# Two fused transformer blocks on one core: partial sums of squares on VectorE, a shorter final norm with stores in pieces, and the last layer's value tiles inside its scan

## The reference, cut to what matters

```python
# block 1, per layer i
mix = jnp.concatenate([conv_out, attn_out], axis=-1) @ w_out[i] + b_out[i]
h = layer_norm(DEEPNORM_ALPHA * h + mix, ln1_g[i], ln1_b[i])       # the norm "ln1_0", "ln1_1"
...
# block 2, per layer: x is the stream, ctx the context, 256 tokens each
xn = rmsnorm(x, norm_g) * (1 + scale_x) + shift_x                  # "rms0", "rms1"
cn = rmsnorm(ctx, norm_g) * (1 + scale_c) + shift_c
aq, ak, av, az, mq, mk, mv, mo, mz, mi, mf = project(xn, w_in)
caq, cak, cav, caz, cmq, cmk, cmv, cmo, cmz, cmi, cmf = project(cn, w_in)
att_x = window_ctx_attention(q, k, v, kc, vc, sink) * jax.nn.silu(az)
h_ctx, ctx_state = mlstm_bidir(cq, ck, cmv, cmi + b_i, cmf + b_f, mlstm_init_state(B))
h_lat, _ = mlstm_bidir(xq, xk, mv, mi + b_i, mf + b_f, ctx_state)
m_x = mlstm_post(h_lat, mo, mz, head_g)
x = x + gate_x * (jnp.concatenate([att_x, m_x], axis=-1) @ w_out)
...
return rmsnorm(x, final_g)                                         # "final"
```

## Time and profile before

| | |
|---|---|
| median of 3 runs | 2153.48 us (2153.09 to 2160.43) |
| the profiled execution's own time | 2151.44 us |
| its span in the trace | 2149.7 us |
| PE matmul busy | 2048.8 us, 95% |
| DVE, ACT busy | 777.3 us (36%), 406.5 us (19%) |
| mean DMA rate | 236 GB/s |
| last layer of block 2 in the trace | from about 1872 us to the end |

### The profile page before, as it was taken

How to read it: one execution, slowest core, us unless ns; L and a number is a source line. 1 busy time by engine, 2 the same in 40 slices (tenths; PEclk the granted TensorE clock), 3 DMA queues, 4 the chain that set the end, 5 groups by cost and what they waited for, 6 DMA issues and landing times.

```text
span 2149.7 us, 36889 instructions
## 1 busy us (share of the span) xinstructions
PE 2048.8 (95%) x15906; PEld 1484.5 (69%) x15906; DVE 777.3 (36%) x1764; ACT 406.5 (19%) x964; POOL 5.8 (0%) x12
## 2 busy tenths in 40 slices
PE   8999999999999999999999999998999898999877
PEld 6879999886776666666666656666645666576776
DVE  6737555595321111111011110113156355335354
ACT  1233110104210111000100000002143423123322
POOL 0000000000000000000000000000000000000000
PEclk9999999999999999999999999999999999999998
DMA  9483444545089999999999999993211111232100
GB/s 314 178 272 136 157 171 183 188 165 196 7 346 393 420 419 417 420 421 420 418 418 420 420 420 420 415 420 165 98 40 59 40 40 40 78 118 74 60 25 20
DMA packets 71940, 506.75 MB, mean 236 GB/s; under 512 B 7776, under 2 KB 9824, under 8 KB 11232
## 3 DMA queue, kind: packets, MB, share of 16 engines
q1 hardware_dynamic: 70624, 500.15, 58.2%
q0 software_dynamic: 1152, 4.19, 0.8%
HBM read 503.27 MB, written 1.05 MB: 235 GB/s over the span
## 4 chain that ended last, share of the span: by engine, by line
PE 89%; DMA 4%; DVE 4%; ACT 2%; issue 1%; DVEq 0%; SPq 0%; ACTq 0%
PE ps L450 87%; DMA work<-weights 2%; DMA ring<-weights 2%; PE ps L1161 1%; PE ps L724 1%; DVE work L2605 1%; ACT work L1771 0%; DMA xc<-x_t 0%; DVE work L2566 0%; PE ps L600 0%; DVE work L2672 0%; DVE work L2562 0%; DVE work L1955 0%; PE ps L1262 0%; DVE work L2563 0%
## 5 line engine op out<-in xcount | busy, mean ns | idle before, releaser
L450 PE MATMUL ps<-work 128*32 128x256 f32 (+8 forms) x5608 | 589.2, 383 | 30.9 <-DVE work L2605 11.3
L450 PE MATMUL ps<-work,ring 128*128 128x256 f32 (+2 forms) x2056 | 520.5, 408 | 6.1 <-DVE work L2672 5.0
L450 PEld LDWEIGHTS ps<-work 128*32 128x32 f32 (+3 forms) x5608 | 380.8, 138 | 196.8 <-issue 122.1
L450 PE MATMUL ps<-ring,work 128*32 128x256 f32 (+3 forms) x4824 | 470.4, 410 | 13.4 <-DMA work<-weights 4.0
L450 PEld LDWEIGHTS ps<-work,ring 128*128 128x128 f32 x2056 | 353.3, 192 | 142.6 <-issue 107.0
L450 PEld LDWEIGHTS ps<-ring,work 128*32 128x32 f32 (+1 forms) x4824 | 261.3, 120 | 148.2 <-issue 75.8
L450 PE MATMUL ps<-xc,ring 128*128 128x256 f32 (+1 forms) x1440 | 277.1, 352 | 5.6 <-DMA ring<-weights 4.0
L450 PEld LDWEIGHTS ps<-xc,ring 128*128 128x128 f32 x1440 | 241.7, 191 | 42.6 <-issue 7.5
L2218 DVE TENSOR_TENSOR work<-work,ps 128x256 f32<-128x256 f32 x42 | 17.7, 421 | 419.6 <-ACT work L1622 419.6
L450 PE MATMUL ps<-xc,work 128*128 128x256 f32 (+1 forms) x720 | 138.3, 350 | 0.0
L450 PEld LDWEIGHTS ps<-xc,work 128*128 128x128 f32 x720 | 120.8, 191 | 19.9 <-issue 3.8
(11 more groups left out here) (273 smaller groups left out, 1169.8 us busy)
## 6 DMA issues: line engine op xcount, KB each, us to landing
ring<-weights SPq DMA_DIRECT2D x317, 1024.0 KB, 12.2
work<-weights SPq DMA_DIRECT2D x154, 1024.0 KB, 16.2
work<-rel POOLq DMA_DIRECT2D x8, 512.0 KB, 9.3
con<-consts SPq DMA_DIRECT2D x1, 1368.0 KB, 21.2
xc<-x_t SPq DMA_DIRECT2D x1, 1024.0 KB, 7.7
xc<-ctx_t SPq DMA_DIRECT2D x1, 1024.0 KB, 25.2
out<-work SPq DMA_DIRECT2D x1, 1024.0 KB, 3.9
par<-params SPq DMA_DIRECT2D x1, 872.0 KB, 9.1
```

Source lines behind the costliest of these rows:

```text
L450: ins = eng.matmul(o, lhs, rhs, start=start, stop=stop, **kw)
```

## The change

Four edits.

1. **Norm ln1, both layers.** While DVE adds the residual (`block1_out`), it also adds up chunks 0 to 6 in `rstd1`, by six additions. PE's mean then takes 2 matmuls with ones, over that sum and over chunk 7, and not 8.
2. **Norms rms1 and final.** While DVE adds the output projection to x (`block2_out`), it also adds up the squares of chunks 0 to 6 in `rstd2`, by six additions, each placed ahead of the next chunk's addition. PE's sum of squares takes 2 matmuls and not 8.
3. **Final norm.** One operation for each chunk, (x * gain) * reciprocal, takes the place of a multiplication and a scaling: 8 operations and not 16. The store is 4 DMAs of 2 chunks (256 KB), each waiting only for its own chunks.
4. **The last layer's stream values.** In layer 1 the value tiles with t = 0, 1 (4 tiles, 8 pieces) leave the attention's filler and become the first filler of the scan. The attention deals 32 pieces and not 40; the scan 28 - 4 = 24 over its 24 steps, and not 16. The scan waits for the other four value tiles at its start, and for these at j = 2. The first `mz` tile of layer 1 uses bank 7.

```diff
+            def norm_mean_summed(l):
+                name = f"ln1_{l}"
+                o = fill(("mean", name), 0, (s["norm_centered"], before(name) + KC))
+                eng.wait_ge(s["res_summed"], (KC - 2) * (l + 1))
+                mm(o[:, 0:T], ones, rstd1, True, False)
+                eng.wait_ge(*source(name, KC - 1))
+                mm(o[:, 0:T], ones, res[:, KC - 1, :], False, True).then_inc(bank_full[0], 1)
+
+            def norm_var_summed(name, summed):
+                o = fill(("var", name), 1, (s["norm_std"], normk(name)))
+                eng.wait_ge(s["sq_summed"], summed)
+                mm(o[:, 0:T], ones, rstd2[:, 0:T], True, False)
+                eng.wait_ge(s["norm_squared"], before(name) + KC)
+                mm(o[:, 0:T], ones, squares(name, False)[:, KC - 1, 0:T], False, True).then_inc(bank_full[1], 1)
...
+        MV_FIRST = ([0, 1, 2, 3], [2, 3])
...
                 for u in range(2):
-                    w = next_unit()
-                    for t in range(4):
-                        o = fill(("mv", l, u, t), t % 2, (s["mv_copied"], 8 * l + 4 * u + t + 1))
+                    w = next_unit(beside=l == 1 and u == 1)
+                    if l:
+                        value_units.append(w)
+                    for k, t in enumerate(MV_FIRST[l]):
+                        o = fill(("mv", l, u, t), t % 2, (s["mv_copied"], 8 * l + len(MV_FIRST[l]) * u + k + 1))
                         yield from token_pieces(("mv", l, u, t), w, t, o, t % 2)
...
             def block2_third(l):
+                if l:
+                    for k in range(4):
+                        u, t = divmod(k, 2)
+                        b = 7 if k else 6
+                        o = fill(("mv", l, u, t), b, (s["mv_copied"], 8 * l + 4 + k + 1))
+                        yield from token_pieces(("mv", l, u, t), value_units[u], t, o, b)
...
-                    b = 7 if c else 6
+                    b = 7 if c or l else 6
...
-                rounds, total = att_rounds(l), 48 if l == 0 else 40
+                rounds, total = att_rounds(l), 48 if l == 0 else 32
...
-                total = (32 if l == 0 else 20) - SCAN_START[l]
+                total = (32 if l == 0 else 28) - SCAN_START[l]
...
-                eng.wait_ge(s["mv_copied"], 8 * (l + 1))
+                eng.wait_ge(s["mv_copied"], 8 * l + 2 * len(MV_FIRST[l]))
                 for j in range(4):
                     rows = has_rows(l, j, 0)
+                    if l and j == 2:
+                        eng.wait_ge(s["mv_copied"], 8 * (l + 1))
...
-            eng.wait_ge(s["norm_out"], outk("final"))
-            eng.dma_start(out, cen).then_inc(s["out_stored"], 16)
-            eng.wait_ge(s["out_stored"], 16)
+            for c in range(0, KC, 2):
+                eng.wait_ge(s["norm_out"], outk("final", c + 1))
+                eng.dma_start(out[:, c:c + 2, :], cen[:, c:c + 2, :]).then_inc(s["out_stored"], 16)
+            eng.wait_ge(s["out_stored"], 16 * KC // 2)
...
+            def final_norm():
+                eng.wait_ge(s["norm_std"], normk("final"))
+                link(eng.reciprocal(rstd2[:, 0:T], std2[:, 0:T]))
+                for c in range(KC):
+                    eng.scalar_tensor_tensor(out=cen[:, c, :], in0=xc[:, c, 0:T], scalar=par[:, PC("final_g", c)],
+                                             in1=rstd2[:, 0:T], op0=ALU.mult, op1=ALU.mult).then_inc(s["norm_out"], 1)
...
+                    if 1 <= c < KC - 1:
+                        eng.wait_ge(s["mix_added"], KC * l + c + 1)
+                        if c > 1:
+                            eng.wait_ge(s["res_summed"], (KC - 2) * l + c - 1)
+                        eng.tensor_tensor(rstd1, rstd1 if c > 1 else res[:, 0, :], res[:, c, :], ALU.add)\
+                            .then_inc(s["res_summed"], 1)
...
+            def sum_squares(l, c):
+                name = ("rms1", "final")[l]
+                had = (KC - 2) * l + c - 1
+                sq = squares(name, False)
+                eng.wait_ge(s["norm_squared"], before(name) + c + 1)
+                if c > 1:
+                    eng.wait_ge(s["sq_summed"], had)
+                eng.tensor_tensor(rstd2[:, 0:T], rstd2[:, 0:T] if c > 1 else sq[:, 0, 0:T], sq[:, c, 0:T], ALU.add)\
+                    .then_inc(s["sq_summed"], 1)
...
+                    if c >= 2:
+                        sum_squares(l, c - 1)
```

More of the change, by code:

```diff
@@ L305, in build @@
         names = """weights_used ones_loaded x_loaded params_loaded late_loaded rel_loaded rel_ready out_stored
-            norm_src norm_centered norm_squared norm_std norm_scaled norm_out norm_out_a coef_out
+            norm_src res_summed sq_summed norm_centered norm_squared norm_std norm_scaled norm_out norm_out_a coef_out
             cond_ready cond_row prep_done glu_gate glu_out qk_out v_out mod_out xo_half x_half conv_mixed
@@ L1116, in block2_second @@
                 for u in range(2):
-                    w = next_unit()
-                    for t in range(4):
-                        o = fill(("mv", l, u, t), t % 2, (s["mv_copied"], 8 * l + 4 * u + t + 1))
+                    w = next_unit(beside=l == 1 and u == 1)
[3 more added lines that the diff above has]
+                        o = fill(("mv", l, u, t), t % 2, (s["mv_copied"], 8 * l + len(MV_FIRST[l]) * u + k + 1))
                         yield from token_pieces(("mv", l, u, t), w, t, o, t % 2)
+            value_units = []
             def block2_third(l):
@@ L1380, in _ @@
                 block1_out(l)
-                norm(f"ln1_{l}", res, KC, T)
+                norm_mean_summed(l)
+                norm_var(f"ln1_{l}", KC, T, True)
                 if l == 0:
@@ L1394, in _ @@
                 if l:
-                    norm("rms1", xc, KC, T, centred=False)
+                    norm_var_summed("rms1", KC - 2)
                     context_var()
@@ L1402, in _ @@
                 block2_out(l, started)
-            norm("final", xc, KC, T, centred=False)
+            norm_var_summed("final", (KC - 2) * 2)
             assert unit_no[0] == UNITS, (unit_no[0], UNITS)
@@ L1727, in block2_second, with value_copy @@
                 for u in range(2):
-                    for t in range(4):
+                    for t in MV_FIRST[l]:
                         yield "mv", l, u, t
-                        o = tile(eng, "mv", l, u, t)
-                        eng.activation(mv[:, t, 2 * u:2 * u + 2, 0:M_DH],
-                                       o[:, 0:GW].rearrange("p (a b) -> p a b", b=M_DH), ACT.Copy)\
-                            .then_inc(s["mv_copied"], 1)
+                        value_copy(l, u, t)
+            def value_copy(l, u, t):
+                o = tile(eng, "mv", l, u, t)
+                eng.activation(mv[:, t, 2 * u:2 * u + 2, 0:M_DH], o[:, 0:GW].rearrange("p (a b) -> p a b", b=M_DH),
+                               ACT.Copy).then_inc(s["mv_copied"], 1)
             def block2_third(l):
@@ L1737, in block2_third @@
                 q_tiles = 4 if l == 0 else 2
+                if l:
+                    for u in range(2):
+                        for t in range(2):
+                            yield "mv", l, u, t
+                            value_copy(l, u, t)
                 for c in range(M_HEADS):
@@ L2799, in _ @@
                 block2_out(l)
-            norm("final", xc, KC, T,
-                 lambda c, a: eng.tensor_scalar(cen[:, c, :], cen[:, c, :], par[:, PC("final_g", c)], None, ALU.mult),
-                 centred=False, dst=cen)
+            final_norm()
 def weight_units(a):
```

## The result

| | before | after |
|---|---|---|
| median of the runs | 2161.10 us (16 runs, 2152.93 to 2176.41) | 2142.46 us (16 runs, 2131.82 to 2151.68) |
| the profiled execution and its span | 2151.44, 2149.7 us | 2139.72, 2137.7 us |

The ratio is 0.9913, with an interval of 0.9891 to 0.9935: faster by 0.9%, or 19 us. The time is 10 us over the one forecast and half a microsecond outside the range. Two things have to be kept apart: what the edits did, and how far the executions of one kernel lie apart. The executions of before cover 23 us, those of after 20 us. The gain itself, 18.6 us between the two medians with an interval of about 14 to 24, holds the 21.25 that was forecast.

The account below looks back on a forecast made before the run. The prediction took TensorE's work and waits as the bound. Norms and store 9.15 us, attention 12.1 and scan 0 sum to 21.25, so 2153.48 became 2132 us, range 2125 to 2142.

Parts of the forecast that it names:

- the base: Whole kernel: the median of before's runs, 2153.48 us, 2.0 above the profiled execution, from which the gain was subtracted.
- The sum: Whole kernel: norms and store 9.15 us, attention 12.1, scan 0, together 21.25 us saved.
- The additions on DVE: Norms: additions of about 0.41 us each hide beside PE's work; without that cover 0.41 at most would show.
- The end: Last square to the span's end: 14.1 us before, less 1.8, 1.6 and 1.0, gives 9.7 after.
- The store's term: Kernel's end: four stores for one save 1.0 us, between 0 and 1.9; by the Trainium skill 1.3.
- The attention: Layer 1 of block 2: eight pieces leave, waits grow 4.4 to 6.4 us, 99.8 becomes 87.7, 12.1 less.
- The scan: Last layer: exposed pieces cost 6.5 us, recovered clock returns 6.7; length stays 87.4 at granted clock 1.00.
- The price put on the filler's bank: Scan: exposed filler pieces wait for ACT's copy of shared bank 7, 0.65 us and 0.75 us.
- Rival 1: Scan: the low clock stays and 6.7 us of the gain is lost, 2139 us; chance 0.20.
- Rival 2: Scan grows by 12 us, eating the attention's gain; only 9.15 remains, 2144 us; chance 0.10.
- Rival 3: Experts: their weight stream ends when it did, losing ln1's 3.6 us, 2136 us; chance 0.10.
- Rival 4: Scan: new fillers keep TensorE at 1.2 GHz, making the kernel slower, 2172 us with half affected; chance 0.02.

Follow-up runs that it names:

- run 9: Kernel after plus one unread matmul in every second round of block 1's attention (12 in all): 2139.41 us median, 6 runs.
- run 11: Kernel before plus one unread matmul in every second round of block 1's attention (12 in all), sent again: 2161.55 us median, 12 runs.
- experiment 8: Kernel after with the result stored once as 1 MB instead of four 256 KB stores: 2149.65 us, one run; last square to end 10.67 us.
- Experiment 4: Kernel after with ACT copying the turned probabilities before a filler tile that ends with the round: 2122.87 us, ratio 0.9823 to before.
- run 6: Kernel before plus one unread matmul in every second round of block 1's attention (12 in all): 2160.32 us, ratio 0.9998.
- experiment 7: Kernel after with turned probabilities copied first, plus layer 1's scan filler tiles alternating between banks 6 and 7: 2125.33 us, ratio 0.9857 to before.
- run 1: Kernel before with only the fourth edit, the last layer's stream values computed in the scan: 2153.71 us, ratio 0.9936.
- run 10: Kernel after with turned probabilities copied first and 12 unread matmuls in block 1's attention: 2120.70 us, ratio 0.981 to before.
- experiment 12: Kernel after with turned probabilities copied first, no unread matmuls, sent again on another chip: 2134.66 us, ratio 0.9873 to before.
- run 5: Kernel before plus one unread matmul in every round of block 1's attention (22 in all): 2164.49 us, ratio 1.0015.

## Why the prediction was right and wrong

**The step that failed is the base.** "The median of the runs is 2.0 us above the profiled one, and I forecast 2153.48 - 21.25" takes three runs for the kernel's time, and allows "some 3 us between executions" in the range. Two of the three runs lay at the fast end: the 16 runs of before beside the result have a median of 2161.10, 7.6 us higher, and that is most of the 10.3 us by which the forecast missed; the other 2.6 lie in the gain, 18.6 for 21.25, and within its interval. The 85 runs of before in this study cover 2151.27 to 2177.97 with a median of 2162.4, and 20 of them are under 2156. From 2162.4 the same sum gives 2141.1, from 2161.10 it gives 2139.9, and 2142.46 was measured.

What makes the spread is the clock. The mean granted clock of the whole execution is known for 69 of these 85 runs: the 15 at 0.988 or more took 2151.27 to 2155.93 us, the 10 at 0.979 or less 2172.47 to 2177.97. Where it falls the profiled executions show. Each fall in block 1's attention costs 8.5 to 10.3 us (13.7 once), and there are two such stages; by an estimate from these, none, one or two falls make 2151, 2161 or 2171, with shorter low stretches elsewhere between. In the nine profiled executions without unread matmuls in that stage the fall is there in 8 of 18 stages; in the five with them, in 0 of 10. The sign was in what was known: the three runs, 2153.09, 2153.48 and 2160.43, were 7 us apart, and nothing in the prediction asked what makes 7 us. The high end of the range should have been 2132 + 10 at least.

**The sum was right.** -21.25 forecast, -21.55 by the stages, -22.1 between runs 9 and 11, -21.1 between the fastest runs beside the result (2131.82 against 2152.93). Term by term:

- ln1: -1.8 each, measured -1.73. rms1: -1.15, measured -1.12. The final sum of squares: -1.8, measured -1.73.
- The additions on DVE were called hidden. In ln1 they are; in rms1 and final they are not, since each stands between PE's chunk and its addition to x: 0.36 is given back in rms1, and the stretch that holds final's is 0.33 us longer. The bound given for the lost cover was 0.41, with the addition of chunk 6 as its reason.
- The end: 9.7 forecast, 9.00 measured. The eight operations are right (3.26 for 3.3). The store's term is mis-sized: -1.0 forecast, -1.7 by experiment 8. The row of a 273.5 KB load, 2.9 us, was too long a stand-in for a 256 KB store, which lands in 2.1. The Trainium skill (DMA: Bandwidth & Descriptors, "Anatomy of one DMA") was closer with -1.3 in all; it states its fit for GpSimd's path, and these stores go by SP's queue. By its figures the 256 KB would take 2.6 us and the 1 MB 4.4, estimates, where the traces show 2.1 and 3.9; the difference is 1.8 by the page and 1.8 by the traces. The bound of -1.9, given as half of the load's time, does not come out of its rows: 4.3 - 0.35 - 1.45 is 2.5. The measured term lies within either.
- The attention: 87.7 forecast, 87.75 measured, with 6.1 us of waits for 6.4 forecast, in the places named. Experiment 4 confirms what makes them.
- The scan: 87.4 forecast, 86.93 measured, PEclk 1.00 and 9.1 us of waits for 9 forecast. By busy and idle time 6.5 us of the pieces are uncovered and 7.0 came back from the clock, for 6.5 and 6.7 forecast. These two are less sure than their difference: other executions with before's scan have a higher PEclk, 0.92, and are 1.7 shorter (85.74 in run 6). By (1 - PEclk) x length before's scan loses up to 8.7 us, so the clock may be worth up to 8.5 and the uncovered pieces 8.0, both estimates. The price put on the filler's bank, 0.65 + 0.75 = 1.4, is 0.8 by experiment 7.

**The rivals.** Rival 1, that the low clock stays: not in the scans of after and of runs 1, 7, 9 and 10; experiments 4, 8 and 12 have one stretch, worth 1.4 (88.3 to 88.4 against 86.93), never three. The Trainium skill's rule on short idle times between groups that go from bank to bank (TensorE: Matmul & The Clock Gate, "A second HAM failure mode: psum-queue depth-cycling") is thus borne out by no more than that one stretch. Rival 2, a longer scan: no, it is 0.5 shorter. Rival 3, the norm's gain lost at the experts: no, 976.16 and 976.27. Rival 4, slower: no.

**What stays open** is why the clock falls in block 1's attention in one execution and not in the next. In runs 5, 6, 9, 10 and 11, with a little more work for PE there, no profiled execution has it; PE's waits ahead of it are equal with and without a fall. That copying the turned probabilities first makes falls more frequent is possible (experiment 12) and not shown: experiment 4's profile has none. Nor can it be told whether the change itself makes falls more frequent: among the executions without unread matmuls there, those with the norm edits have 6 in 12 stages and those without 2 in 6. The Trainium skill (TensorE: Matmul & The Clock Gate, "What's actually happening") says that one kernel can show a differing number of matmuls at low clock from run to run, and says it of a kernel's start; here it is 100 and 500 us into the kernel.

## What to carry to other kernels

Before a difference is forecast, ask how far the runs of the kernel before lie apart, and look for the stretch that makes it; two of three runs can lie at one end, and a base that is off by 8 us spoils a sum that is right to 1. Where PE waits for a chain on another engine, work moved into the waits can be nearly free, and part of the pay is the clock that it keeps up. When two versions must be told apart by less than the spread, put the same unread matmuls into the stretch that flickers in both: here 6 and 12 runs then gave 22 us (17 to 28), where 16 and 16 without them had given 19 (14 to 24).

## What the runs showed of the hardware

- TensorE's granted clock fell to 0.50 for about 17 to 27 us in a stage where PE was over 80% busy in windows of 10 us, in 8 of 18 chances, at 8.5 to 13.7 us each, and in 0 of 10 with one matmul of 256 columns more in every round or every second round.
- 14.1 us of unread matmuls in a scan with 16.7 us of PE's waits changed the kernel's time by a ratio of 1.0002 (0.9974 to 1.003), and the granted clock of the scan was 0.98 with them and 0.90 without.
- On SP's queue a store of 256 KB landed 2.1 us after its issue, one of 1 MB 3.9.
